# Second layer's weight sums on POOL: the third and fourth sum of a unit one step of the scan later

## What is computed

```python
proj = jnp.einsum('bsd,df->bsf', h, w_in)
q, f_f, f_b, i, gate = _split(proj, (C_WIDTH,) * 5)
f = lb + (1.0 - lb) * jax.nn.sigmoid(z)          # for f_f and f_b: key 1 - f, log decay log f
o = bidirectional_gated_scan(silu(q) * C_HEAD_DIM ** -0.5, k_f, g_f, k_b, g_b, heads(i))
y = _head_rmsnorm(o, norm_gain) * jax.nn.silu(gate)
```

## Time and profile before

| | |
|---|---|
| median of 3 runs | 4165.31 us (4161.42 to 4167.26) |
| profiled execution | 4166.81 us |
| its span | 4165.1 us |
| PE busy | 3590.4 us, 86% of the span |
| POOL busy | 1183.5 us, 28% |
| DVE busy | 1780.1 us, 43% |
| TensorE's granted clock, mean | 0.92 |
| POOL's queries of this stage, L810 | 292.0 us in 192, mean 1540 ns |

### The profile page before, as it was taken

How to read it: one execution, slowest core, us unless ns; L and a number is a source line. 1 busy time by engine, 2 the same in 40 slices (tenths; PEclk the granted TensorE clock), 3 DMA queues, 4 the chain that set the end, 5 groups by cost and what they waited for, 6 DMA issues and landing times. The chain is left out here.

```text
span 4165.1 us, 46995 instructions
## 1 busy us (share of the span) xinstructions
PE 3590.4 (86%) x16369; PEld 2345.8 (56%) x16369; DVE 1780.1 (43%) x4038; ACT 1075.4 (26%) x2201; POOL 1183.5 (28%) x940
## 2 busy tenths in 40 slices
PE   8899998889698999999978598998985776958996
PEld 4645776667343666675645444756665776434442
DVE  0025552443353365566566353133467577240101
ACT  1023343332232223223233242121212212211111
POOL 0000000333243355555456355000313436211110
PEclk9999999899899999999989798899997788979998
DMA  3254632231541111211111533214234631446996
GB/s 113 82 165 141 172 107 79 76 97 46 199 164 51 54 54 49 60 54 42 55 46 37 223 132 95 50 37 123 85 96 122 227 132 34 174 168 237 311 326 229
DMA packets 408273, 494.01 MB, mean 119 GB/s; under 512 B 70499, under 2 KB 314491, under 8 KB 408052
## 3 DMA queue, kind: packets, MB, share of 16 engines
q1 hardware_dynamic: 379431, 457.42, 33.1%
q0 software_dynamic: 4608, 16.78, 1.6%
q10 hardware_dynamic: 24012, 16.97, 1.3%
HBM read 362.32 MB, written 128.77 MB: 118 GB/s over the span
## 5 line engine op out<-in xcount | busy, mean ns | idle before, releaser
L810 POOL TENSOR_TENSOR hgrn_queries<-hgrn_qd,hgrn_pair_decay 128x640 f32<-128x640 f32 x192 | 292.0, 1540 | 329.7 <-PE hgrn_ps_a L921 321.6
L856 PE MATMUL hgrn_ps_w<-xT,hgrn_ring 128*128 128x512 f32 x432 | 196.6, 601 | 8.0 <-DMA hgrn_ring<-in_w_in_c_dram 8.0
L395 PE MATMUL gla_bg_ps<-gla_bg_w,xT 128*128 128x256 f32 x768 | 196.0, 402 | 4.6 <-DMA gla_bg_w<-in_w_in_ab_dram 4.6
L395 PEld LDWEIGHTS gla_bg_ps<-gla_bg_w,xT 128*128 128x128 f32 x768 | 151.6, 202 | 38.0 <-issue 10.6
L1424 PE MATMUL end_ps_z<-end_w,end_yT 128*128 128x512 f32 x384 | 169.7, 602 | 1.6 <-ACT end_yT L1373 1.6
L2511 PE MATMUL end_ps_z<-end_w,end_yT 128*128 128x512 f32 x384 | 166.9, 594 | 0.8 <-ACT end_yT L2439 0.8
L391 PE MATMUL att_bg_ps<-xT,att_bg_w 128*128 128x512 f32 (+1 forms) x288 | 136.8, 615 | 13.3 <-POOL att_ident L1731 13.3
L856 PEld LDWEIGHTS hgrn_ps_w<-xT,hgrn_ring 128*128 128x128 f32 x432 | 81.9, 194 | 100.7 <-issue 92.1
L45 POOL MEMSET gla_ident<- 128x128 f32 x1 | 0.2, 204 | 484.8 <-POOLq L34 484.8
L861 PE MATMUL hgrn_ps_w<-hgrn_ring,xT 128*128 128x256 f32 x576 | 132.5, 387 | 0.0
L856 PE MATMUL hgrn_ps_w<-hgrn_xs,hgrn_wsum 128*128 128x512 f32 x288 | 128.2, 592 | 0.0
(11 more groups left out here) (643 smaller groups left out, 7759.8 us busy)
## 6 DMA issues: line engine op xcount, KB each, us to landing
expw_wg<-in_exp_w_gate_dram SPq DMA_DIRECT2D x16, 2048.0 KB, 9.7
expw_wu<-in_exp_w_up_dram SPq DMA_DIRECT2D x16, 2048.0 KB, 16.3
expw_wd<-in_exp_w_down_dram SPq DMA_DIRECT2D x16, 2048.0 KB, 21.8
att_w_ada<-in_ada_w_dram SPq DMA_DIRECT2D x24, 1024.0 KB, 6.1
hgrn_ring<-in_w_in_c_dram SPq DMA_DIRECT2D x18, 1024.0 KB, 5.4
end_gt<-gate_l SPq DMA_DIRECT2D x16, 768.0 KB, 7.9
hgrn_ring<-in_w_in_c_dram SPq DMA_DIRECT2D x24, 512.0 KB, 5.3
hgrn_o<-hgrn_o_stage SPq DMA_DIRECT2D x192, 64.0 KB, 1.6
```

What stands on the lines that cost most here:

```text
L395: last = pe.matmul(bank[0:job.rows, q * job.width:(q + 1) * job.width], job.acts[:, k, t * P:t * P + job.rows], w[:, k, 0:job.width], star ...
L810: pool.tensor_tensor(queries[:, d, s, :].rearrange("p (b a c) -> p b a c", b=POINTS, a=PC), q, f, ALU.mult).then_inc(queries_done, 1)
L856: last = pe.matmul(bank[:, :], a[:, k, :], x(k), start=(fresh and k == 0), stop=(k == HK - 1), skip_group_check=True)
```

## The change

The first two sums of a unit stay where they were. The third gets a function of its own, `sum_third`, and a step of its own in a table `third_at`: one step after the first two, though not later than one step after the step of the fill that needs it. The late sum goes one step later where the step of its fill LAST allows. In a step, the loop over units keeps the order first, second, third, late for each unit. `sum_third` has the drain that stood before the third sum, and no wait on a semaphore.

```diff
+        e = 0 if u == LEAD_UNITS else step_of[prev - 3] + 2
+        t = max(e, min(e + 1, step_of[first_fill[u] + 2] + 1))
+        early_at.setdefault(e, []).append(u)
+        third_at.setdefault(t, []).append(u)
+        late_at.setdefault(max(t, step_of[prev] + 2, min(step_of[prev] + 3, step_of[first_fill[u] + 6])), []).append(u)
...
                 pool.tensor_tensor(weights_of(u, 1, 0), weights_of(u, 1, 0), weights_of(u, 1, 1), ALU.add).then_inc(s_made, 1)
+
+            def sum_third(u):
+
                 pool.drain()
                 pool.tensor_tensor(sum_of(u, 1), weights_of(u, 1, 0), weights_of(u, 0, 0), ALU.subtract).then_inc(s_made, 1)
...
-                for u in late_at.get(g, ()):
-                    sums_late(u)
-                if g:
-                    for u in early_at.get(g, ()):
+                for u in range(LEAD_UNITS, len(units)):
+                    if g and u in early_at.get(g, ()):
                         sums_early(u)
+                    if u in third_at.get(g, ()):
+                        sum_third(u)
+                    if u in late_at.get(g, ()):
+                        sums_late(u)
```

More of the change, by code:

```diff
@@ L563, in projected_scan @@
     LEAD_UNITS = spans[0][1]
-    early_at, late_at = {}, {}
+    early_at, third_at, late_at = {}, {}, {}
     for u in range(LEAD_UNITS, len(units)):
         prev = last_fill[u - 1]
-        early_at.setdefault(0 if u == LEAD_UNITS else step_of[prev - 3] + 2, []).append(u)
-        late_at.setdefault(step_of[prev] + 2, []).append(u)
+        e = 0 if u == LEAD_UNITS else step_of[prev - 3] + 2
[3 more added lines that the diff above has]
+        late_at.setdefault(max(t, step_of[prev] + 2, min(step_of[prev] + 3, step_of[first_fill[u] + 6])), []).append(u)
     for (kind, n), u in unit_at.items():
@@ L768, in _ @@
             sums_early(0)
+            sum_third(0)
             sums_late(0)
@@ L816, in _ @@
             sums_early(3)
+            sum_third(3)
             scale_keys_in(0, 1)
```

## The result

The changed kernel takes **4182.72 us** (median of five runs, 4175.67 to 4189.80) against 4167.26 us for the kernel before in the same session (five runs, 4161.42 to 4171.96). The ratio is 1.0038, interval 1.0023 to 1.0053: slower by 15.5 us. The forecast was +13 us, 4178 us. The profiled execution took 4182.72 us.

A forecast was written before the change was run, and what follows sets the result against it. TensorE (PE) was taken to bound the second layer's scan. Wide units 7.6, narrow units 1.6 and units 20 to 23 +4 us sum to +13 us on a median of 4165.31: 4178 us, own range 4170 to 4187, range of all 4158 to 4190.

The forecast's parts named there:

- First chain of the wide units: Units 5, 9, 13, 17: one POOL operation less meets DVE's chain to k_end, 9.36 for 11.26 us; PE waits 2.6, not 4.50.
- Second chain: Wide units, 12.01 us later: the late sum behind POOL's keys blocks DVE's L997, so k_end comes 2.2 us later.
- The clock behind it: Behind the wide units' second k_end: low PE clock takes 1.9 us a unit, less 0.3 for a sooner state update.
- locks only: Rival (a): the clock behaves no worse than before; +6 us in all, 4171 us; chance 0.34.
- Narrow units: Units 7, 11, 15, 19, third sum behind queries and keys: +0.2 us order, +0.2 us clock each, +1.6 us in all.
- Units 6 and 8 and their like at nothing: Units 6, 10, 14, 18 and 8, 12, 16: PE's two fills a step cover DVE, so no cost.
- The last heads: Units 20 to 23, where fills are sparse and PE catches DVE: sum +4 us, between -2 and +6.
- three times 1.2 us: Late sums of units 20 and 21 and third of 22 move before an awaited k_end: 1.2 us each, half a wide sum.
- Unit 21's third sum: Leaves the k_end at 2130.58, which takes 1.50 instead of 0.49 us: -1.0 us.
- Unit 23's late sum: 2.4 us long, leaves the front of step 82's queries but lands before k_end: +1.5 us.
- Rival "faster": Rival (b): POOL starts the late sum over 1 us behind the keys, k_end gets in first; -16 us, 4149 us; chance 0.11.
- Rival "late for PE": Rival (c): late sums make PE stand at fills, up to 2.5 us at ten places, +25 us, 4190; chance 0.05.

The follow-up runs named there:

- x4_wide2: Against the kernel before, in units 5, 9, 13, 17 alone the third sum one step and the late sum two steps later: 4165.93 against 4169.81 us, ratio 0.9991.
- x7_memset: The changed kernel with the late sum of units 5, 9, 13, 17 replaced by two memsets: 4167.86 us against 4170.49 for the kernel before, ratio 0.9993.
- x5_narrow: Against the kernel before, third and late sum one step later in units 7, 11, 15, 19 alone: 4170.53 against 4170.49 us, ratio 1.0003.
- x9_tail: Against the kernel before, third and late sum one step later in units 20 to 23 alone: 4173.42 against 4170.20 us, ratio 1.0010.
- x6_both: Against the kernel before, units 5, 9, 13, 17: third sum one, late two steps later; 7, 11, 15, 19: third two steps later. 4154.31 us, ratio 0.9964.
- x0_null: The kernel before, unchanged, executed once more: 4168.17 us.

## Why the prediction was right, term by term

The sum was right, +13 us forecast, +15.5 measured by the medians and 12.7 in the stage's three stretches. The mechanism was the one forecast: the queries come free and PE doesn't profit, because what it awaits is the chain behind. Only the wide units' term, 7.6 of the 13 us, stands clear of chance in the runs. The narrow units' 1.6 us can't be told from nothing, and in the last heads the clock adds and takes up to 1.7 us at single steps that no term names. That the whole came so near is in part luck.

- **First chain of the wide units.** One lock less: 9.36 us forecast, 9.35 measured; PE's wait 2.6 us forecast, 2.60, 2.59, 2.58 and 2.60 measured.
- **Second chain.** +2.2 us forecast, 11.51 − 9.36 = 2.15 measured. The waits are 3.22, 3.70, 3.46 and 4.74 us, "3 or 4" in the text. From the queries' front to the second k_end PE needs 17.08 us (1463.14 to 1480.22) for 17.00 before: the locks alone cost 0.1 us at this unit, +0.3 in the forecast.
- **The clock behind it.** Forecast 1.9 − 0.3 = 1.6 us a unit. At unit 5 it is 1.64 us, 10.26 us from the second k_end to the next front (1480.22 to 1490.48) for 8.62 (1478.49 to 1487.11). Over the four units locks and clock are 8.7 us for the 7.6 of the forecast, unevenly, from 1.56 to 2.73 us. x4_wide2 and x7_memset, with 1.07 and 1.08 us of wait in its place, need 8.62 us for that stretch, as before. The rival "locks only" (+6 us in all) fell on this term.
- **Narrow units.** +1.6 us forecast; 3.8 us in the changed kernel's profile, 2.6 in x5_narrow's, of which the kernel before against itself shows 2.5. The forecast isn't contradicted, and it can't be told from nothing. At unit 7 the wait for queries of 0.75 us is gone and the wait for k_end is 4.26 us for 3.28, 0.23 us more than both waits before, where the text has 0.2. POOL's third sum meets `ends` there as forecast, POOL's row first, then DVE's:
```profile
1561.63 1.26 POOL L765 TENSOR_TENSOR hgrn_wsum<-hgrn_ring 128x512 f32<-128x512 f32 x1 [0.16 <-issue]
```
```profile
1561.68 1.26 DVE L1008 TENSOR_TENSOR hgrn_ends<-hgrn_totals,hgrn_points 128x32 f32<-128x32 f32 x1
```
- **Units 6 and 8 and their like at nothing.** Right: all other steps of the spans agree within 0.03 us.
- **The last heads: a little less than forecast**, +4 us against 2.6 (changed kernel, measured against the second execution of the kernel before) and 2.7 (x9_tail) in the profiles. The term "three times 1.2 us" was mis-sized: in PE's waits unit 20's late sum gave +0.89 (1.24 for 0.35 us), unit 21's late sum +0.87 (1.25 for 0.38, x9_tail) and unit 22's third sum +1.07 (3.35 for 2.28, x9_tail), 2.8 us for 3.6. In the changed kernel's profile the wait at unit 22 is 1.67 us, because the clock had cost PE 1.68 us just before it; x6_both, whose sum isn't moved there, has the same 1.68 and a wait of 0.59, again 1.08 less. Unit 21's third sum gave −1.06 us (6.47 for 7.53), −1.0 forecast, but the unchanged kernel's second execution has 6.87 there. All seven profiles with this sum in its old place have 6.87 to 7.92, all five with it moved 5.63 to 6.53. Unit 23's late sum stands before k_end itself (DVE, then PE):
```profile
2252.21 2.46 DVE L1035 TENSOR_TENSOR hgrn_k_end<-hgrn_kd,hgrn_end_decay 128x128 f32<-128x128 f32 x2
```
```profile
2254.72 0.44 PE L907 MATMUL hgrn_ps_a<-hgrn_ident,hgrn_k_end 128*128 128x128 f32 x2 [2.30 <-DVE hgrn_k_end L1035]
```
PE waits 2.30 us for k_end where it didn't wait, and 0.87 us come back with the queries' wait. In x9_tail that is +1.50 us net, just the +1.5 of the forecast. In the changed kernel the low clock comes behind this wait, step 82 takes 9.60 us for 5.58, and 0.66 us come back in the next two steps, where PE would have waited anyway (0.48 and 1.15 us before): +2.49 us net. The prediction had no clock in this term. The 1.60 us that step 85 is shorter don't belong to it: they go with step 89, as said above.
- **Rival "faster", −16 us.** Its deciding point was a start of POOL over 1 us behind the keys. POOL starts 0.16 us behind them, and the late sum wins by 0.05 us (1476.55 against 1476.60). The place that the rival described does pay: with the late sum out of both wide chains and one sum out of the narrow one, x6_both is 16 us faster. That this is the rival's own number is chance, since only 10 to 12.5 us of it lie at those units.
- **Rival "late for PE"**: there is no wait of PE for wsum.

## What to carry to other kernels

Moving a POOL operation out of the way of what POOL itself delivers helps only if that delivery is what the bounding engine awaits; look first at which wait ends last. In these rows a POOL tensor operation that reads SBUF, begun just ahead of a DVE operation with two SBUF inputs, holds it to its own end, once: 2.34 us for an operation of 0.19, so the question for each place is which DVE operation it will meet and how much slack stands behind that chain. A move from a chain with a long wait into one that was just in time gains nothing and can put the low clock where no slack absorbs it; move it on, into a step in which the bounding engine has work of its own.

## What I had not expected of the hardware

**The clock behind a wait is not a function of that wait.** In the kernel before, the transposes behind a wait of 4.51 us at 1632.05 take 0.69 us; in another execution of the same program those behind the 4.50 us at 1635.07 take 0.44 (timelines of before, then of x0_null):
```profile
1632.05 0.69 PE L896 MATMUL hgrn_ps_a<-hgrn_ident,hgrn_k_end 128*128 128x128 f32 x2 [4.51 <-DVE hgrn_k_end L1024]
```
```profile
1635.07 0.44 PE L896 MATMUL hgrn_ps_a<-hgrn_ident,hgrn_k_end 128*128 128x128 f32 x2 [4.50 <-DVE hgrn_k_end L1024]
```
In the second the clock fell all the same, by the next row (1.01 us for four small matmuls, granted clock 0.60 from 1635 to 1637), and the steps around it differ by only 0.17 us. More hangs on how long the low level lasts. At the last narrow unit the same two executions have the same waits, 0.75 and 3.28 us, and transposes of 0.69 us behind them; but the fill that follows runs at full speed in the first and not in the second, and the step is 1.64 us longer:
```profile
2062.22 3.60 PE L856 MATMUL hgrn_ps_w<-xT,hgrn_wsum 128*128 128x512 f32 x8
```
```profile
2065.84 5.12 PE L856 MATMUL hgrn_ps_w<-xT,hgrn_wsum 128*128 128x512 f32 x8
```
Step 89 above is another case: the same 2.62 us of wait, and 1.68 us more in five profiles of twelve, the five in which the low clock of step 85 ended sooner. In the changed kernel the first waits of 2.59 and 2.58 us have transposes of 0.69 us behind them, those of 2.60 and 2.60 us 0.44. I have no rule from these runs for which of the two comes.

**How exactly the rest repeats.** In the four spans, over 650 us, all steps outside 4 to 6 and 12 to 14 agree within 0.03 us in all twelve profiles. A loss of 2 us can thus be placed from one profile of each kernel wherever no long wait stands; at a long wait it must come back at every unit of its kind to count. The total of one run scatters by 10 us and more, in good part behind the stage (1835.5 to 1851.9 us).
